# The opening of a two-layer streaming encoder step: one cached-latent block moves to the other transfer queue, ScalarE's order is turned, a warm-up product is halved

## The reference, cut to what matters

```python
kv = (c_kv @ w_kvup).reshape(B, K, MLA_HEADS, MLA_NOPE_DIM + MLA_V_DIM)
k_nope, v = kv[..., :MLA_NOPE_DIM], kv[..., MLA_NOPE_DIM:]
k = rmsnorm(jnp.concatenate([k_nope, kr], axis=-1), qk_k_norm)
```

## Time and profile before

| | us |
|---|---|
| median of 3 runs | 1043.76 |
| lowest and highest run | 1043.03, 1043.83 |
| the profiled execution, its own time | 1046.98 |
| its span, from the first to the last instruction | 1045.2 |
| TensorE busy | 1038.1 (99%) |
| VectorE busy | 643.9 (62%) |
| ScalarE busy | 506.6 (48%) |
| GpSimd busy | 314.5 (30%) |

### The profile page before, as it was taken

The page is one execution under the profiler, slowest core; times in us unless marked ns, Lnnn a source line. Parts: engine busy times, 40 slices in busy tenths (PEclk is TensorE's granted clock), DMA queues, the critical chain, the costliest instruction groups (busy, mean ns, idle before and its releaser), DMA issues.

```text
span 1045.2 us, 20057 instructions
## 1 busy us (share of the span) xinstructions
PE 1038.1 (99%) x7572; PEld 1003.7 (96%) x7572; DVE 643.9 (62%) x1093; ACT 506.6 (48%) x936; POOL 314.5 (30%) x277
## 2 busy tenths in 40 slices
PE   8999999999999999999999999999999999999998
PEld 6899999999999999999988999999999999999998
DVE  6889764445766666543567996554557565565443
ACT  6567755444554444434354585554445444433341
POOL 2365566531221111100132755656312211111000
PEclk9999999999999999999999999999999999999999
DMA  6465533334535444454513544334344354444541
GB/s 223 114 166 139 186 103 121 92 131 142 161 121 166 156 145 156 142 179 146 176 46 117 167 147 139 94 117 122 122 152 152 122 179 141 155 146 145 158 148 64
DMA packets 49146, 146.27 MB, mean 140 GB/s; under 512 B 8792, under 2 KB 14904, under 8 KB 49080
## 3 DMA queue, kind: packets, MB, share of 16 engines
q1 hardware_dynamic: 42464, 142.86, 43.8%
q10 hardware_dynamic: 6616, 2.50, 1.0%
HBM read 142.11 MB, written 3.22 MB: 139 GB/s over the span
## 4 chain that ended last, share of the span: by engine, by line
PE 98%; DVE 1%; issue 1%; ACT 0%; POOL 0%; ACTq 0%; POOLq 0%
PE psum L585 29%; PE psum L586 29%; PE psum L587 29%; PE psum L786 1%; PE psum L825 1%; PE psum L808 1%; PE psum L816 1%; PE psum L858 1%; PE psum L1047 0%; PE psum L913 0%; PE psum L948 0%; PE psum L687 0%; PE psum L850 0%; PE psum L729 0%; PE psum L722 0%
## 5 line engine op out<-in xcount | busy, mean ns | idle before, releaser
L585 PE MATMUL psum<-AH,WH 128*128 128x320 f32 x1328 | 414.3, 312 | 0.2
L587 PE MATMUL psum<-AH,WL 128*128 128x320 f32 x1328 | 410.3, 309 | 0.0
L586 PE MATMUL psum<-AL,WH 128*128 128x320 f32 x1328 | 410.2, 309 | 0.0
L585 PEld LDWEIGHTS psum<-AH,WH 128*128 128x128 f32 x1328 | 249.2, 188 | 7.4 <-issue 5.5
L586 PEld LDWEIGHTS psum<-AL,WH 128*128 128x128 f32 x1328 | 249.3, 188 | 0.2
L587 PEld LDWEIGHTS psum<-AH,WL 128*128 128x128 f32 x1328 | 249.3, 188 | 0.0
L1130 ACT CAST WH<-raw 128x1024 fp32r<-128x1024 f32 x166 | 172.7, 1045 | 123.2 <-PE psum L587 122.4
L1603 DVE TENSOR_TENSOR WL<-raw,WH 128x1024 fp32r<-128x1024 f32 x103 | 128.9, 1252 | 113.4 <-ACT WH L1130 113.1
L2094 POOL TENSOR_TENSOR WL<-raw,WH 128x1024 fp32r<-128x1024 f32 x60 | 147.7, 2478 | 97.7 <-ACT WH L1130 94.8
L1802 DVE TENSOR_TENSOR WL<-raw,WH 128x1024 fp32r<-128x1024 f32 x88 | 107.5, 1222 | 49.6 <-ACT WH L1313 48.3
L2099 POOL TENSOR_TENSOR fab<-fa,fb 128x320 f32<-128x320 f32 x44 | 38.7, 879 | 264.7 <-DVE fb L1807 264.7
(11 more groups left out here) (296 smaller groups left out, 1580.4 us busy)
## 6 DMA issues: line engine op xcount, KB each, us to landing
raw<-w_all SPq DMA_DIRECT2D x264, 512.0 KB, 3.5
y_out<-X SPq DMA_DIRECT2D x8, 160.0 KB, 2.7
X<-x_in SPq DMA_DIRECT2D x2, 320.0 KB, 5.2
X<-x_in SPq DMA_DIRECT2D x1, 640.0 KB, 7.1
lat_out<-ckv ACTq DMA_DIRECT2D x2, 320.0 KB, 2.9
scratch<-brel SPq DMA_DIRECT2D x8, 63.8 KB, 4.2
bias<-scratch SPq DMA_DIRECT2D x8, 48.0 KB, 3.9
ckv<-lat_in ACTq DMA_DIRECT2D x1, 384.0 KB, 4.5
```

Source lines behind the costliest of these rows:

```text
L585: mm(out, WH[:, slot, c0:c0 + cols], high, start=first, stop=False)
L586: mm(out, WH[:, slot, c0:c0 + cols], low, start=False, stop=False)
L587: return mm(out, WL[:, slot, c0:c0 + cols], high, start=False, stop=last)
```

## The change

Three edits, all in the opening.

1. SyncE's second transfer is now the latents of block 0, between the value and the key weights, and the latents of block 1 are no longer on its list.
2. ScalarE begins with the wait for `warm_zero` and the square root with its table load, then issues the rotary keys, then the latents of block 1. The casts follow as before.
3. The last of the four warm-up products has 160 columns instead of 320.

```diff
         sp.dma_start(raw[:, U_KVV, :], w_all[stored(U_KVV)]).then_inc(raw_ready[U_KVV], 16)
+        sp.dma_start(ckv[:, :, T:T + 128], lat[:, :, 0:128]).then_inc(s.cache_lat[0], 16)
         sp.dma_start(raw[:, U_KVK, :], w_all[stored(U_KVK)]).then_inc(raw_ready[U_KVK], 16)
-        sp.dma_start(ckv[:, :, T + 128:T + 256], lat[:, :, 128:256]).then_inc(s.cache_lat[1], 16)
         sp.dma_start(cst[:, K_ID:K_ID + 128], cst_in[:, K_ID:K_ID + 128]).then_inc(s.id_in, 16)
...
         pe.wait_ge(s.warm_zero, 1)
-        for _ in range(WARM):
-            mm(psum[:, tbank(3), 0:T], ssum[:, 0:128], ssum[:], start=True, stop=True)
+        for n in range(WARM):
+            cols = T if n < WARM - 1 else T // 2
+            mm(psum[:, tbank(3), 0:cols], ssum[:, 0:128], ssum[:, 0:cols], start=True, stop=True)
...
-        act.dma_start(ckv[:, :, T:T + 128], lat_in[0:1].rearrange("a p c n -> (a p) c n")[:, :, 0:128]) \
-            .then_inc(s.cache_lat[0], 16)
-        rope_cached(0)
         act.wait_ge(s.warm_zero, 1)
         A(small[:, 31:32], ssum[:, 0:1], ACT.Sqrt)
+        rope_cached(0)
+        act.dma_start(ckv[:, :, T + 128:T + 256], lat_in[0:1].rearrange("a p c n -> (a p) c n")[:, :, 128:256]) \
+            .then_inc(s.cache_lat[1], 16)
         act.wait_ge(raw_ready[U_KVV], 16)
```

## The result

| | before, us | after, us |
|---|---|---|
| median of 12 runs each | 1043.80 (1042.67 to 1044.21) | 1045.09 (1044.79 to 1048.01) |
| profiled execution, own time | 1046.98 | 1044.79 |
| its span | 1045.2 | 1042.9 |

A forecast was written before the change was run, and what follows sets the result against it. TensorE, busy 1038.1 of 1045.2 us, was taken as the bound, leaving only opening waits and slow clock. Gains of 2.3 (parts 1 and 2) and 0 (part 3) took 1043.76 to 1041.5, forecast as 1041.67, range 1040.3 to 1043.3.

The forecast's parts named there:

- part 1: Opening: block 0's latents, issued behind the value weights, land at 5.2, so TensorE starts at 6.1 instead of 7.96.
- Sum: Whole kernel: 2.3 us gained by part 1 and part 2 together, 0 by part 3; forecast 1041.67.
- late next: Opening: key weights, queued behind 128 KB, land at 7.2 (6.7 to 7.9); key rows end about 9.5 at full clock.
- The clock: Block 0's value and key rows: end 9.5 at full clock, 10.7 if mostly low; 9.9 taken, 2.3 us gained.
- part 2: ScalarE's opening: table load from 0.75 to 2.05 overlaps the issues; block 1's latents land at 8.6, hidden.
- part 3: Warm-up: halving the last product takes 0.58 us off but saves nothing directly, as TensorE waits for latents until 6.1.
- Does the gain reach the end: After the squares: a shift of 2.3 us passes whole; one above 2.9 would be cut at weight unit 2.
- block 1's latents become the wait: Rival before ScalarE's squares: these latents land at 9.7 or 10.0, gain 1.5 or 1.2 us, time 1042.5; chance 0.14.
- the clock stays low through the rows: Rival in block 0's value and key rows: they end at 10.7, gain 1.5 us, time 1042.3; chance 0.15.
- they land far later: Rival before ScalarE's squares: block 1's latents land beyond 11.2, making the kernel slower; 1046.0 at 13.5; chance 0.04.
- the late engine: Rival in the opening: block 0's latents land near 7 from either queue, gain 0 to 0.7 us, 1043.4; chance 0.11.
- slower: Whole kernel: the outcome that the change makes it slower by over 0.2%; chance 0.03.

The follow-up runs named there:

- e2: The changed kernel run again with no edit; median 1045.18 us, ratio 1.0011 to the kernel before.
- e3: The changed kernel with the last warm-up product back at its full 320 columns; median 1045.07 us, ratio 1.0014 to the kernel before.
- e1: The kernel before run and profiled again with no edit; median 1043.96 us, ratio 1.0001.
- e10: The kernel before with SyncE's issue of the key weights held from 1.20 to about 1.95; median 1044.78 us, ratio 1.0009.
- e8: The changed kernel with block 0's latents behind the key weights instead of in front; median 1047.32 us, ratio 1.0036 to the kernel before.
- e7: The kernel before with only ScalarE's order turned: table load and root before block 0's latents and the rotary keys; median 1044.96 us, ratio 1.0020.
- e9: The changed kernel with the rotary keys issued only after GpSimd's memset; median 1045.09 us, ratio 1.0014 to the kernel before.
- e4: The kernel before with only the last warm-up product halved; median 1043.87 us, ratio 1.0000.
- e13: The kernel before with the key weights' issue held to 1.45, an earlier release than in e10; median 1044.00 us, ratio 0.9994.
- e6: The kernel before with 128 KB of weight unit 3 moved between the value and key weights; median 1045.31 us, ratio 1.0015.
- e12: The kernel before with the edits of e7 and e10 joined; median 1047.77 us, ratio 1.0031.
- e16: One more execution of e12's kernel, no edit, on another chip; 1044.81 us.
- e17: A further single execution of e12's kernel, no edit, on another chip than e12's; 1044.97 us.
- e15: e12's kernel with the rotary keys also held until GpSimd's memset is done; median 1047.48 us, ratio 1.0028 to the kernel before.
- e11: The kernel before with the rotary keys issued only behind the table load and GpSimd's memset; median 1043.69 us, ratio 1.0000.

## Why the prediction was wrong

**The base of the sum (part 1, and "Sum").** The prediction set the change against one execution that lay 3.22 us above the median, said so, and moved the saving over: "the same saving from 1043.76 makes 1041.5". That is the step that failed. For the profiled execution its sum came out right: 1044.7 forecast, 1044.79 found, by way of a split at 5.3 (4.99), value rows at 6.1 (5.85), keys at 7.2 (7.43), squares at 9.9 (9.97). That is in part luck, since e2 and e3, with the same transfers, had their squares at 11.41 and 11.80. But the usual execution of before had no gap of 2 us for the change to close. Its squares begin at 8.86 in e1 (9.0 by the estimate from the median), and from e1's to the changed kernel's 9.97 is a loss of 1.1 us. The 3.2 us between the profile and the median were the late landings (7.10 and 7.37 against 4.64 and 6.11) and the half clock behind them: between the two executions of the same code the squares differ by 3.4 us and the times by 3.6.

**The key weights ("late next").** Weighed by bytes in front of them: 7.2, with 7.9 as the late end. The 7.43 lies inside, but the comparison did not: 7.37 was taken for the usual landing, which is 6.1. What was left out is the issue itself. The latents' issue takes 0.68 us of SyncE and moves that of the key weights from 1.20 to 1.93. I charged bytes and no time of issue; e10, where no bytes are put in front of them on their queue, brings them to 7.40. Whether it is the time that counts or what the other queue has issued by then, and why 0.73 us of issue become 1.3 of landing, is not settled.

**The clock.** The dip of the earlier trace rows is missing in e1 and in the profile after. It came in executions with late latents: TensorE idle for 2.05 us, then the lower level (in e8 idle for 2.80 us, then 0.51). The change did not remove such rows for good: in e2 and e3 they ran at half speed, as shown above. The price of this case was mis-added: with 0.43 us each until 9.4 and 0.23 after it, twelve products from 6.1 end at about 10.4, not 10.7. The rule of the Trainium skill (TensorE: Matmul & The Clock Gate, Part 1), that the full clock comes at another point from run to run, was kept for the ends of the range. The traces agree with it: in the same program the products start 0.23 us apart from 6.16 on (the profile after) or only from 10.04 on (e2). It was the hint that one profile's opening is a sample.

**ScalarE's order (part 2).** Right as to the table load: it ran from 0.75 to 2.03, and the first issue went out beside it at 1.25; the second followed at 2.68, as the first took 1.39 us and not 1.12. Right that block 1's latents would not be the wait: cast at 8.48 straight behind the casts of the weights. Alone, in e7, the order costs 1.0020, as block 0's latents land late (6.28); in the change they are on the other queue, and moving the rotary keys away (e9) gives nothing back.

**The halved product (part 3).** Costed at nothing: e4, 1.0000.

**Does the gain reach the end.** The shift passed whole in the profile: line 585 starts at 22.55, 12.6 us behind the squares, as forecast, and the 1034.5 to 1034.9 us of all executions say the same.

**The rivals.** That block 1's latents become the wait, that the clock stays low through the rows and that they land far later were each given a chance; none is the usual case. Two of them showed in the slowest executions: e2 and e3 have latents after 6, towards the late engine, and rows at half speed, the clock's. No rival had the cause found here, the key weights later than usual by the changed place of their issue. For the direction, slower got 0.03.

## What to carry to other kernels

When the profiled execution is off the median of the runs by more than the effect in question, first find where that difference sits; here all 3.2 us were the wait that the change was to remove and the half clock behind it. A transfer put in front of another costs the issuing engine's time as well as bytes. Here 128 KB in front, 0.57 us by bytes at the late end, cost the landing 1.3 us against e1, and holding the issue with no bytes in front cost the same. Profile the same kernel again before reading any row, and take an execution that lies on the median of the runs; a second one can be off it as well (e2, e3).

## What the runs showed of the hardware that was not expected

- Landings in the first 8 us are not proportional to the time of issue. 512 KB issued at 1.20 or 1.45 were read at 6.11 and 6.12, issued at 1.93 at 7.40 (e1, e13, e10), and issued at 1.66 behind another transfer at 8.45 (e6). 128 KB issued at 0.75 and at 1.25 were read at 4.64 and 6.28 (e1, e7).
- Neither order nor time of issue is a rule by itself. Latents at 1.25 behind keys at 1.20 were read at 6.28, in front of keys at 1.94 at 4.80, 5.00 and 5.70 (e7; e12, e16, e17), but in e15, with the same order and the same times of these two, at 7.20.
- The same program's opening varies by 3.4 us from execution to execution with no edit (squares at 8.86 and 12.24), while the 12 runs of its first measurement lie within 1.5 us (1042.67 to 1044.21) and the profiled one outside them.
- The products of the rows can run at half speed where the column of the granted clock says 1.00 (e2: starts 0.42 us apart instead of 0.23).
- No version tried beat the kernel before by more than its interval; the nearest are e11 (1.0000) and e13 (0.9994, 0.9985 to 1.0004).
